# A two-layer transformer forward pass in 3-term fp32: norm boundaries in two blocks of time steps, down products summed block by block, value tiles first

## What is computed

```python
def rmsnorm(x, g):
    xf = x.astype(jnp.float32)
    y = xf * lax.rsqrt(jnp.mean(xf * xf, axis=-1, keepdims=True) + EPS)
    return (y * g.astype(jnp.float32)).astype(x.dtype)

def conv_ffn(h, w_up, conv_w, w_down):
    u = causal_dwconv(h @ w_up, conv_w)
    a, g = jnp.split(u, 2, axis=-1)
    return (jax.nn.silu(a) * g) @ w_down

for layer in range(DEPTH):
    if layer < N_A:
        x = x + short_conv_mixer(rmsnorm(x, mix_norm[layer]), a_w_in[i], a_conv[i], a_w_out[i])
    else:
        if layer == N_A:
            kv = nsa_shared_kv(rmsnorm(x, kv_norm), w_kv, cmp_pe, cmp_w1, cmp_b1, cmp_w2)
        x = x + nsa_mixer(rmsnorm(x, mix_norm[layer]), b_w_qg[i], b_w_o[i], kv, rel_bias)
    x = x + conv_ffn(rmsnorm(x, ffn_norm[layer]), ffn_up[layer], ffn_conv[layer], ffn_down[layer])
return rmsnorm(x, final_norm)
```

## Time and profile before

| | us |
|---|---|
| three runs | 636.45, 636.32, 636.69 |
| median | 636.45 |
| profiled execution | 635.05 |
| its span | 633.3 |
| PE busy | 612.2 (97%) |
| DVE busy | 485.3 (77%) |
| ACT busy | 388.6 (61%) |
| POOL busy | 59.4 (9%) |

### The profile page before, as it was taken

The page is one execution under the profiler, slowest core; times in us unless marked ns, Lnnn a source line. Parts: engine busy times, 40 slices in busy tenths (PEclk is TensorE's granted clock), DMA queues, the critical chain, the costliest instruction groups (busy, mean ns, idle before and its releaser), DMA issues.

```text
span 633.3 us, 11277 instructions
## 1 busy us (share of the span) xinstructions
PE 612.2 (97%) x3738; PEld 531.8 (84%) x3738; DVE 485.3 (77%) x939; ACT 388.6 (61%) x708; POOL 59.4 (9%) x78
## 2 busy tenths in 40 slices
PE   7999999999999999999999888998999999999995
PEld 7999997888888888888989766777888888888884
DVE  4787756888888777777878789837788887777865
ACT  6645436666666666658556478717766666656644
POOL 0110011000000000011131144421000000000010
PEclk9999999999999999999999999999999999999999
DMA  8797432565655555761476400033355655555521
GB/s 313 283 334 241 181 132 100 184 212 198 203 200 199 184 182 181 290 224 35 148 255 206 136 2 2 1 101 132 138 209 190 219 205 193 178 175 186 199 100 66
DMA packets 30640, 109.55 MB, mean 173 GB/s; under 512 B 3419, under 2 KB 3691, under 8 KB 30476
## 3 DMA queue, kind: packets, MB, share of 16 engines
q1 hardware_dynamic: 30044, 106.97, 48.1%
q0 software_dynamic: 560, 2.12, 1.0%
HBM read 108.00 MB, written 1.07 MB: 172 GB/s over the span
## 4 chain that ended last, share of the span: by engine, by line
PE 88%; DVE 5%; ACT 3%; issue 2%; POOL 1%; DMA 1%; SPq 0%; DVEq 0%; ACTq 0%
PE bank L1109 26%; PE bank L1090 15%; PE bank L1091 14%; PE bank L1092 14%; PE bank L1110 13%; POOL work L486 1%; DMA staged<-in_a_up 1%; DVE work L1013 1%; PE bank L1356 1%; ACT work L533 1%; PE bank L1314 1%; PE bank L1144 1%; ACT w_hi L529 1%; PE bank L1316 0%; ACT L508 0%
## 5 line engine op out<-in xcount | busy, mean ns | idle before, releaser
L746 DVE TENSOR_TENSOR w_lo<-staged,w_hi 128x1024 fp32r<-128x1024 f32 x191 | 236.7, 1248 | 42.1 <-ACT w_hi L529 42.0
L1109 PE MATMUL bank<-gx,w_hi 128*128 128x512 f32 x704 | 249.7, 398 | 0.9 <-DVE gx L820 0.9
L529 ACT ACTIVATE w_hi<-staged 128x1024 fp32r<-128x1024 f32 x197 | 199.4, 1046 | 25.1 <-PE bank L1092 15.7
L1110 PE MATMUL bank<-gx,w_lo 128*128 128x256 f32 x704 | 197.7, 281 | 0.0
L1109 PEld LDWEIGHTS bank<-gx,w_hi 128*128 128x128 f32 x704 | 132.3, 188 | 33.0 <-issue 1.3
L1110 PEld LDWEIGHTS bank<-gx,w_lo 128*128 128x128 f32 x704 | 133.3, 189 | 1.5
L1091 PE MATMUL bank<-w_lo,y 128*128 128x512 f32 x208 | 81.6, 392 | 0.0
L1090 PE MATMUL bank<-w_hi,y 128*128 128x512 f32 x208 | 81.5, 392 | 0.0
L1092 PE MATMUL bank<-w_hi,y 128*128 128x512 f32 x208 | 81.0, 390 | 0.0
L615 ACT ACTIVATE work<-work,params 128x256 f32<-128x256 f32 x96 | 44.2, 504 | 56.9 <-DVE work L847 39.2
L1090 PE MATMUL bank<-gx,w_hi 128*128 128x256 f32 x256 | 72.9, 285 | 3.2 <-DVE w_lo L746 2.7
(11 more groups left out here) (156 smaller groups left out, 785.8 us busy)
## 6 DMA issues: line engine op xcount, KB each, us to landing
staged<-in_f_up SPq DMA_DIRECT2D x88, 512.0 KB, 5.2
staged<-in_f_down SPq DMA_DIRECT2D x44, 512.0 KB, 3.3
staged<-in_a_up SPq DMA_DIRECT2D x24, 512.0 KB, 7.0
staged<-in_b_up SPq DMA_DIRECT2D x24, 512.0 KB, 4.0
staged<-in_a_down SPq DMA_DIRECT2D x8, 512.0 KB, 3.4
staged<-in_b_down SPq DMA_DIRECT2D x8, 512.0 KB, 4.2
bias<-bias_rows POOLq DMA_DIRECT2D x1, 2048.0 KB, 12.0
bias<-in_xT SPq DMA_DIRECT2D x4, 256.0 KB, 5.5
```

The lines of the kernel that those rows point to most:

```text
L529: nc.scalar.activation(w_hi[:, q["slot"], 0:n], staged[:, s, 0:n], ACT.Copy).then_inc(hi, 1)
L746: nc.vector.tensor_tensor(w_lo[:, q["slot"], 0:n], staged[:, s, 0:n], w_hi[:, q["slot"], 0:n].bitcast(F32), ALU.subtract).then_inc(lo, 1)
L1109: nc.tensor.matmul(out_ap, w_hi[:, s, cols], gx[:, kt, :], start=start, stop=False, skip_group_check=True)
L1110: return nc.tensor.matmul(out_ap[:, 0:T], w_lo[:, s, cols], gx_hi[:, kt, :], start=False, stop=stop, skip_group_check=True)
```

## The change

The norms are done block by block, and the stages around them are written so that PE has products to do meanwhile.

- `last_two` sums the last two units of every stage (a, f0, f1 and the output product of b) so that both banks of block 0 are finished first, then the two of block 1. The last unit's y is needed after two banks' share of the unit before it.
- `last_step` replaces the last `step` of an FFN: half c = 0 goes up to its silu before half c = 1 is copied out of PSUM.
- In `norm`, ACT and DVE do block 0 up to gx_hi and gx_lo (16 instructions of 128 columns in place of 8 of 256 for each of them over both blocks), then block 1. KEEP_WARM is gone.
- `units_0_1` replaces `unit_0` and the up product of unit 1: matmuls of 512 columns become two of 2 x 128 columns, one for each block (`wide_half`), and the 256-column ones (`narrow`) come behind. Between block 0 and block 1 of unit 0 stand block 0 of unit 1's first tile and the transposes of block 1.
- In b, the value tiles lead `B_ORDER`; they have the activations as the stationary side and so can be done by block. The cmp and key tiles, the copies out of PSUM and POOL's blocks follow later.
- The split of the last f1 tile of `WHILE_O` moves from before the norm of f1 to behind its ladder on ACT.
- In the last norm, the first half of the output is scaled before `half(1)`.

The transposes of block 1 stand behind 24 half matmuls. The diff, cut to its core:

```diff
-B_ORDER = ([("cmp", t) for t in range(4)] + [("key", t) for t in range(4)] + [("val", t) for t in range(4)]
+B_ORDER = ([("val", t) for t in range(4)] + [("cmp", t) for t in range(4)] + [("key", t) for t in range(4)]
...
+                squares_of(0)
+                squares_of(1)
+                root(0)
...
+                turned_half(0)
+                squares_of(2)
+                squares_of(3)
+                root(1)
+                turned_half(1)
+                if st == "f1":
+                    lead(*WHILE_O[-1])
...
+            def last_step(st):
+
+                k = FU - 1
+                r, at = k % 3, UP[st] + 2 * (k % 2)
+                for c in range(2):
+                    act.wait_ge(used_up, piece_of(st, "up", k, c)["n"] + 1)
+                    nc.scalar.activation(shifted[:, r, c, 2:2 + T], bank[at + c][:, T:2 * T], ACT.Copy).then_inc(lo_read[st], 1)
+                    act.wait_ge(scaled[st], k + 1 + c)
+                    nc.scalar.activation(conv[:, r, c, :], shifted[:, r, c, 2:2 + T], ACT.Copy, scale=tap(st, c, 0, k, 2)).then_inc(tapped[st], 1)
+                    if c == 0:
+
+                        act.wait_ge(convolved[st], 4 * k + 2)
+                        nc.scalar.activation(conv[:, r, 0, :], conv[:, r, 0, :], ACT.Silu).then_inc(silued[st], 1)
...
+                residual(st, 0)
+                residual(st, 1)
+                half(st, 0)
                 if st == "end":
+                    residual(st, 2)
+                    residual(st, 3)
+                    inverse(st, 0)
+                    dve.wait_ge(final_landed, 16)
+                    finals(0)
+                    half(st, 1)
+                    inverse(st, 1)
+                    finals(1)
                     return
...
+                residual(st, 2)
+                scale(0)
+                residual(st, 3)
+                rests(0)
+                half(st, 1)
+                scale(1)
+                rests(1)
...
-                for n in range(KEEP_WARM):
-                    nc.tensor.matmul(bank[ACC_BEFORE[st]][:, 0:P], ones[:], ones[:], start=True, stop=True)
...
+                for kt in range(KT):
+                    pe.wait_ge(gx_lo_done, split_of(st, 0, kt))
                     for c in range(2):
...
+                        wide_half(st, 0, c, 0, kt)
+
+                pe.wait_ge(x_new, 4 * NORM[st])
+                leads_of(1, 0)
+                for kt in range(KT):
+                    wide_half(st, 1, 0, 0, kt)
+                turn_x(st, 1)
...
+                for n in range(2):
+                    if ready is not None:
+                        ready(n)
+                    for h in range(2):
+                        mm = part(n, 0, h)
+                        if n == 1:
+                            mm.then_inc(acc_done, 1)
+                part(0, 1, 0)
+                part(1, 1, 0).then_inc(acc_done, 1)
+                part(0, 1, 1).then_inc(done, 1)
+                part(1, 1, 1).then_inc(done, 1)
```

More of the change, by code:

```diff
@@ L725, in _ @@
                 lead_heads(i)
-            for q in WHILE_O:
+            for q in WHILE_O[:-1]:
                 lead(*q)
@@ new lines, in turn_x @@
+                if t:
+                    pe.wait_ge(gx_lo_done, split_of(st, 0, KT - 1))
+                for c in range(4):
+                    if c == 3:
+                        pe.wait_ge(xn_far, 2 * (k - 1) + t + 1)
+                    else:
+                        pe.wait_ge(xn_done, 6 * (k - 1) + 3 * t + c + 1)
+                    for a in range(2):
+                        mm = nc.tensor.transpose(turned_x(st, 4 * a + c)[:, t * P:t * P + P], xn[:, t, a, c, :], ident[:])
+                    mm.then_inc(x_turned, 1)
@@ new lines, in wide_half, with narrow @@
+            def wide_half(st, k, c, t, kt):
+                out_ap, x_ap = (ap.rearrange("p (a t) -> p a t", a=2)[:, :, t * P:t * P + P]
+                                for ap in (bank[UP[st] + 2 * k + c], gx[:, kt, :]))
+                s = piece_of(st, "up", k, c)["slot"]
+                nc.tensor.matmul(out_ap, w_hi[:, s, kt * P:kt * P + P], x_ap, start=t == 0 and kt == 0, stop=False,
+                                 skip_group_check=True)
+            def narrow(st, k, c):
+                s = piece_of(st, "up", k, c)["slot"]
+                for kt in range(KT):
+                    mm = nc.tensor.matmul(bank[UP[st] + 2 * k + c][:, 0:T], w_lo[:, s, kt * P:kt * P + P], gx_hi[:, kt, :],
+                                          start=False, stop=kt == KT - 1, skip_group_check=True)
+                mm.then_inc(used_up, 1)
@@ new lines, in values @@
+            def values(tt):
+                for t in range(4):
+                    q = piece_of("b", "up", B_ORDER.index(("val", t)), 0)
+                    pe.wait_ge(lo_up, q["n"] + 1)
+                    if tt == 0 and t == 3:
+                        turn_x("b", 1)
+                    for kk in range(2):
+                        kt = 2 * t + kk
+                        pe.wait_ge(gx_lo_done, split_of("b", tt, kt))
+                        mm = three(bank[tt][:], gx_hi[:, kt, tt * P:tt * P + P], gx_lo[:, kt, tt * P:tt * P + P],
+                                   w_hi[:, q["slot"], kk * 512:kk * 512 + 512], w_lo[:, q["slot"], kk * 512:kk * 512 + 512],
+                                   kt == 0, kt == KT - 1)
+                    if tt == 1:
+                        mm.then_inc(used_up, 1)
@@ L1181, in share, with last_two, part, last_downs @@
                 return mm
+            def last_two(acc, tiles, done, ready=None):
+                def part(n, t, h):
+                    s, yh, yl = tiles[n]
+                    cols, ws = slice(t * P, t * P + P), slice(h * 512, h * 512 + 512)
+                    return three(bank[acc + 2 * t + h], yh[:, cols], yl[:, cols], w_hi[:, s, ws], w_lo[:, s, ws], False, n == 1)
+                for n in range(2):
+                    if ready is not None:
+                        ready(n)
+                    for h in range(2):
+                        mm = part(n, 0, h)
[5 more added lines that the diff above has]
+                part(1, 1, 1).then_inc(done, 1)
+            def last_downs(st):
+                units = (AU if st == "a" else FU) - 2
+                ring = 2 if st == "a" else 3
+                def ready(n):
+                    pe.wait_ge(y_lo_done[st], units + n + 1)
+                    pe.wait_ge(lo_down, piece_of(st, "down", units + n, 0)["n"] + 1)
+                tiles = []
+                for k in (units, units + 1):
+                    cols = slice(k % ring * T, k % ring * T + T)
+                    tiles.append((piece_of(st, "down", k, 0)["slot"], y_hi[:, cols], y_lo[:, cols]))
+                last_two(ACC[st], tiles, used_down, ready)
             def down(st, k, i=0):
@@ L1231, in stage @@
                     up_f(st, FU - 1)
-                    for k in range(FU - 3, FU):
-                        down(st, k)
+                    down(st, FU - 3)
+                    last_downs(st)
             pe.wait_ge(consts_done, 1)
@@ L1295, in _ @@
                 pe.wait_ge(lo_up, q["n"] + 1)
[L1296 removed]
+                if what == "w1":
+                    j = t // 2
                     if t == 0:
                         pe.wait_ge(gq_lo_done, 8)
[L1301 to L1308 removed]
                     if t % 2 == 0:
@@ L1422, in _ @@
             attend(HEADS // 2 - 1)
-            for i in range(4, 8):
-                project(i)
+            project(4)
+            project(5)
+            pe.wait_ge(o_lo_done, 8)
+            pe.wait_ge(lo_up, piece_of("b", "up", O_FIRST + 7, 0)["n"] + 1)
+            last_two(ACC["b"], [(piece_of("b", "up", O_FIRST + i, 0)["slot"], gx_hi[:, i, :], gx_lo[:, i, :]) for i in (6, 7)], used_up)
             stage("f1")
```

188 lines of the change are left out of this document (95 added, 93 removed).

## The result

| | before | after |
|---|---|---|
| median of 20 runs each | 635.85 | 637.07 |
| lowest to highest | 634.47 to 636.69 | 635.99 to 640.5 |
| ratio, 95% interval | | 1.0024 (1.0016 to 1.0032) |
| profiled execution, span | 635.05, 633.3 | 637.11, 635.3 |

The changed kernel is 0.24% **slower**, about 1.2 us on the medians. The interval lies clear of 1. The time is inside the range of the prediction, but the sum said 0.45 us sooner and it came 1.2 later: 1.7 us are missing, so that it lies in the range is luck and does not speak for the working. (The 636.0 of the prediction also rested on three runs of the kernel before with a median of 636.45; all 20 give 635.85.)

What follows compares the result with a forecast made beforehand. TensorE is busy almost everywhere, so only its idle stretches or added work move the time. Terms 0.1 (f0) + 0.0 (b) - 0.8 (f1) + 0.25 (end) = -0.45 us gave 636.0, range 634.2 to 638.6.

Steps and rivals of the forecast that it cites:

- Half rungs: Norm ladders writing gx_hi and gx_lo: each 128-column instruction takes 0.256 us on ACT, 0.257 on DVE, instead of 0.361 and 0.393.
- rival 3: Half-width ladder instructions in the norms cost more, as each waits on the other engine: slower, 638 to 639; 18 in 100.
- Half matmuls: Units 0 and 1 of f0 and f1: 96 matmuls of 256 columns at 0.12 us each, adding 0.4 us per stage.
- Boundary a to f0: Norm between stage a and f0: block 0 restarts at 104.9 against 107.26, yet unit 2 starts 0.1 us later.
- A: Slot end at which both residual blocks of steps 0 to 127 are done; PE restarts 4.35 us after it.
- Boundary b to f1: Norm between b and f1: block 0 restarts at 438.85 against 442.25, unit 2 starts 0.8 us sooner.
- the 0.35 for DVE being at a split: Norm of f1: PE's restart comes 0.35 us later because DVE is at a tile split until about 434.0.
- The last y: FFN ends: last y wanted 1.36 us earlier; PE waits 1.5 us for it in f0, none in f1.
- The rival that I named for this step: End of f0: the last y is not late, the 1.5 us wait goes and b starts sooner: 634.5; 12 in 100.
- End: Last norm: half(1) behind the first two final products on DVE makes the last pair start 0.25 us later.
- Clock: Without the warming matmuls at the norms, PE's clock does not fall; rival that it falls: 645, 3 in 100.

Runs made afterwards that it cites:

- e4: The kernel before with only the split of the last f1 tile moved behind the norm of f1 on ScalarE: 634.74, ratio 0.9980.
- e1: The changed kernel with POOL splitting only 64 of 1024 columns of its down tiles in f0 and f1: 634.46, ratio 0.9986 to the kernel before.

## Why the prediction was right and wrong

**Half rungs: right.** 0.256 and 0.257 were predicted from rows of other lines at the same sizes. Measured were 0.257 on ACT and (2.15 - 0.34) / 7 = 0.259 on DVE:

```profile
104.75 2.18 ACT L590 ACTIVATE gx<-bank,params 128x128 fp32r<-128x128 f32 x8 [0.38 <-PE bank L1220]
...
105.25 2.15 DVE L848 SCALAR_TENSOR_TENSOR gx<-bank,params,gx 128x128 fp32r<-128x128 f32 x8
```

With that rival 3 fell: the waits on either side of a rung add nothing that shows here.

**Half matmuls: right.** 0.12 each. From the restart at 105.74, 4.72 for block 1, 2.06 of ladder and 56 x 0.12 come to 119.24; unit 2 started at 119.33. By the Trainium skill's isolated gap (TensorE: Matmul & The Clock Gate, Back-to-back issue gap) it would have been 118.6, an estimate, and no run here shows that pace.

**Boundary a to f0: right**, 0.0 against +0.1. Block 0 restarts 4.23 behind A (predicted 4.35), block 1 4.72 behind that (4.85), and what was gained on block 0 is given back as told.

**Boundary b to f1: right in kind, short in size**, -1.33 against -0.8. The moved split's share is 1.0 at the first matmul, as e4 shows. PE restarts at 440.42; worked out was 438.85, or 440.86 with b's output product 2.01 later, so the 0.35 for DVE being at a split did not show. From there unit 2 comes after 13.69 (13.63 and a hand-over were predicted). Unit 2 waits for DVE's line 903 behind the splits, as predicted:

```profile
453.38 0.68 DVE L903 TENSOR_TENSOR work<-bank,work 128x512 f32<-128x512 f32 x1
```

**The last y: the step that failed.** In the chain that gave y_lo at 288.84, the two multiply-adds of half 0 were priced at 0.48 each, from rows in which DVE had SBUF to itself, and nothing was put in for what ran beside them: the working named the tile split that ACT finishes at 282.3 and forgot who takes it on, POOL, which starts on it at once. In the kernel before, POOL's split and the multiply-adds are 0.6 us apart. `last_step` moves the multiply-adds 1.8 us forward against the split, and that puts the first under it: 1.45 instead of 0.48. For f0 that is 0.9 on top of the 1.5, and it goes straight to b: +0.97 for 0.0. For f1, where the prediction had y 0.04 us ahead of its need, 1.34 instead of 0.48 makes a wait of 0.73 (623.32 to 624.05); with 0.14 of a slower pace in the matmuls behind it, that is +0.88 for 0. Together 1.85, against the 1.7 that are missing between -0.45 and about +1.2; f1's larger gain makes up for small things elsewhere. That b's first w1 tile comes 46.65 after the last downs in e1, where the prediction left the 46.60 of before unchanged, says that the rest of the step was right. The kernel with POOL's split cut short shows the cause, the one with old FFN ends shows the mend. The rival that I named for this step went the other way (y less late), and no rival named it later.

**End: right**, +0.19 against +0.25; `half(1)` behind the first final products costs it, and moving it gives back more than was lost.

**Clock: wrong for one place.** I took from one trace that 2.44 us of waiting at the start leaves the clock alone. In eight profiles with waits of 1.7 to 3.5 us it fell in four. The changed kernel's code at the start is the same, and since "before" has both groups of times as well, the prediction's difference was not touched by it, but single profiles were, by 0.9 us, more than most terms of the sum.

## What to carry to other kernels

When a change moves instructions in time, list what runs beside them on every engine at their new place, and for DVE's operations with two SBUF inputs look at POOL above all: an overlap costs about what is left of POOL's operation, here 1 us from a move of 1.8. An order that wants its input sooner pays only where there is work behind it to bring forward, so try the parts of such a change one by one; here one moved line and one constant gave 1.6 to 1.8 us, and the two new pieces at the FFN ends took away more than the work by blocks gave. Where the terms are under a microsecond, compare distances between marks inside the trace, not spans, since the start alone differs by 0.9 between profiles of the same code.

## What the runs showed of the hardware

- A DVE operation with two SBUF inputs that started under one of POOL's operations of 2.3 to 2.9 us on SBUF ended the same time after POOL's end: 1.09, 1.09 for 1024 columns (1.22 alone), 0.28, 0.28 for 256 columns (0.48 alone). An add with one input in PSUM and ACT's copies are not held. I had this price nowhere in the sum.
- After a wait of 1.9 to 3.5 us at the start, PE's granted clock went to its lower level for some 3 us in four profiles, and after 1.7 to 2.9 us it stayed up in four; after waits of 0.2 to 1.2 us it stayed up in all five. Cost: 0.9 us on average.
- The time of a 128-column operation from PSUM (0.257 on ACT, 0.259 on DVE) could be read to some 2 ns from rows of quite another part of the kernel.
